# Gate and up products of the five FFNs: one 512-column matmul over high and low activations in place of two of 256

## The reference, cut to what matters

```python
def swiglu(h, w_gate, w_up, w_down):          # D_MODEL = 1024, D_FF = 2816, four times
    return (jax.nn.silu(h @ w_gate) * (h @ w_up)) @ w_down
...
        h = _causal_depthwise_conv(x @ w_up[l], conv_w[l], conv_b[l])   # 3 taps, once
        a, u = jnp.split(h, 2, axis=-1)
        ffn = (jax.nn.gelu(a, approximate=False) * u) @ w_down[l]
```

## Time and profile before

| | us |
|---|---|
| timed runs, median of 3 | 1504.58 (1501.1 to 1508.84) |
| span of the profiled execution | 1502.6 |
| TensorE matmuls busy in it | 1390.1 |
| VectorE busy | 883.2 |
| ScalarE busy | 641.9 |

### The profile page before, as it was taken

The page is one execution under the profiler, slowest core; times in us unless marked ns, Lnnn a source line. Parts: engine busy times, 40 slices in busy tenths (PEclk is TensorE's granted clock), DMA queues, the critical chain, the costliest instruction groups (busy, mean ns, idle before and its releaser), DMA issues.

```text
span 1502.6 us, 22505 instructions
## 1 busy us (share of the span) xinstructions
PE 1390.1 (93%) x9058; PEld 1276.6 (85%) x9058; DVE 883.2 (59%) x1146; ACT 641.9 (43%) x767; POOL 185.2 (12%) x196
## 2 busy tenths in 40 slices
PE   6999988898899989999889889999979999799996
PEld 6999976788799989999788769999968887699996
DVE  5445467765455565454556755445486747776667
ACT  4443443544343344434435544433436432354552
POOL 1100004008497000000000000000021310000000
PEclk9999998679999999999999999999989969899998
DMA  8755542229855536555454136555633322555551
GB/s 270 228 181 182 195 138 87 70 59 178 212 191 192 189 123 213 180 183 193 142 166 136 63 99 210 196 175 188 192 97 106 113 71 83 169 175 191 193 180 43
DMA packets 166339, 234.94 MB, mean 156 GB/s; under 512 B 4915, under 2 KB 134082, under 8 KB 166160
## 3 DMA queue, kind: packets, MB, share of 16 engines
q1 hardware_dynamic: 161792, 221.33, 45.6%
q0 software_dynamic: 4496, 12.91, 4.3%
HBM read 233.17 MB, written 1.05 MB: 156 GB/s over the span
## 4 chain that ended last, share of the span: by engine, by line
PE 84%; DVE 9%; ACT 2%; DMA 2%; issue 2%; SPq 0%; DVEq 0%; ACTq 0%
PE ps L304 27%; PE ps L305 26%; PE ps L306 26%; DMA raw<-in_ffn_w_gate_dram 2%; PE ps L834 1%; DVE w_lo L272 1%; PE ps L415 1%; PE ps L1460 1%; DMA raw<-in_ffn_w_up_dram 1%; ACT w_hi L264 1%; DVE h_lo L460 0%; DVE x_tok L1164 0%; DVE h_lo L977 0%; DVE p_sb L921 0%; DVE x_tok L1163 0%
## 5 line engine op out<-in xcount | busy, mean ns | idle before, releaser
L272 DVE TENSOR_TENSOR w_lo<-raw,w_hi 128x2048 fp32r<-128x2048 f32 x209 | 487.1, 2334 | 281.1 <-ACT w_hi L264 281.0
L304 PE MATMUL ps<-h_hi,w_hi 128*128 128x256 f32 x2016 | 578.3, 287 | 12.7 <-DVE w_lo L272 5.0
L305 PE MATMUL ps<-h_hi,w_lo 128*128 128x256 f32 x2016 | 576.0, 286 | 0.0
L306 PE MATMUL ps<-h_lo,w_hi 128*128 128x256 f32 x2016 | 575.7, 286 | 0.0
L264 ACT ACTIVATE w_hi<-raw 128x2048 fp32r<-128x2048 f32 x209 | 398.9, 1910 | 334.3 <-PE ps L306 301.4
L304 PEld LDWEIGHTS ps<-h_hi,w_hi 128*128 128x128 f32 x2016 | 392.9, 195 | 18.5 <-issue 10.8
L305 PEld LDWEIGHTS ps<-h_hi,w_lo 128*128 128x128 f32 x2016 | 393.0, 195 | 1.7
L306 PEld LDWEIGHTS ps<-h_lo,w_hi 128*128 128x128 f32 x2016 | 392.5, 195 | 0.0
L304 PE MATMUL ps<-w_hi,gu_hi 128*128 128x512 f32 x400 | 156.3, 391 | 1.2 <-DVE w_lo L272 1.2
L305 PE MATMUL ps<-w_hi,gu_lo 128*128 128x512 f32 x400 | 156.2, 391 | 0.0
L306 PE MATMUL ps<-w_lo,gu_hi 128*128 128x512 f32 x400 | 155.6, 389 | 0.0
(11 more groups left out here) (249 smaller groups left out, 1311.1 us busy)
## 6 DMA issues: line engine op xcount, KB each, us to landing
raw<-in_ffn_w_gate_dram SPq DMA_DIRECT2D x44, 1024.0 KB, 5.3
raw<-in_ffn_w_up_dram SPq DMA_DIRECT2D x44, 1024.0 KB, 5.4
raw<-in_ffn_w_down_dram SPq DMA_DIRECT2D x44, 1024.0 KB, 4.9
raw<-in_w_up_dram SPq DMA_DIRECT2D x22, 1024.0 KB, 5.1
raw<-in_w_in_dram SPq DMA_DIRECT2D x14, 1024.0 KB, 5.3
raw<-in_odd_w_qkv_dram SPq DMA_DIRECT2D x12, 1024.0 KB, 5.2
raw<-in_w_down_dram SPq DMA_DIRECT2D x11, 1024.0 KB, 4.9
raw<-in_even_w_in_dram SPq DMA_DIRECT2D x6, 1024.0 KB, 5.2
```

The costliest lines, as they stand in the source:

```text
L272: dve.tensor_tensor(w_lo[slot][:, :], raw[slot][:, :], w_hi[slot][:, :].bitcast(F32), ALU.subtract).then_inc(w_lo_ready, 1)
L304: mm(o, ahi, bhi, start=first, stop=False)
L305: mm(o, alo, bhi, start=False, stop=False)
L306: return mm(o, ahi, blo, start=False, stop=last)
```

## The change

h_hi and h_lo become two halves of one tile, h_both, so that one matmul can stream both: 256 columns of hi, then 256 of lo. In the FFNs' gate and up units a new `wide_unit` replaces `feat_unit`. Per (t, k) it streams h_both through the high weights into a whole bank of 512 columns, and h_hi through the low weights into that bank's first half. A bank's two halves must then be added. ScalarE copies the second halves of two banks (t = 0 and 1) to SBUF (`act_part`), and VectorE adds the first halves to them (`dve_sum`). Gate takes banks 0 and 1, up takes 2 and 3. In the plain FFNs gate's sum is in ffn_part (p_sb's second half) and up's in ffn_up; in the conv FFN both go through ffn_part, and all taps read it there instead of PSUM. The order of the splits is changed round these. The projections keep `feat_unit`.

```diff
-        h_hi = sb("h_hi", [P, KC, S], F32R)
-        h_lo = sb("h_lo", [P, KC, S], F32R)
+        h_both = sb("h_both", [P, 2, KC, S], F32R)
+        h_hi, h_lo = h_both[:, 0], h_both[:, 1]
...
+        def wide_unit(pe, n, banks, i=0, ready=None):
...
+            for t in range(2):
+                for k in range(KC):
...
+                    pe.matmul(PS[:, banks + t, :], a[:, k, f], h_both[:, :, k, :], start=k == 0, stop=False)
+                    last = pe.matmul(PS[:, banks + t, 0:S], b[:, k, f], h_hi[:, k, :], start=False, stop=k == KC - 1)
+            last.then_inc(w_released, 1)
...
                 if free is not None:
-                    if self.conv:
-                        pe.wait_ge(self.a_conv if which == 0 else self.u_conv, free)
-                    else:
-                        pe.wait_ge(self.act_done if which == 0 else self.gu_done, free + self.b)
-                feat_unit(pe, n, which, i)
...
+                    pe.wait_ge(self.summed, 2 * free + (2 * self.b + which - 1))
+                wide_unit(pe, n, 2 * which, i)
+
+            def act_part(self, act, which, i, at, dst):
...
                 act.wait_ge(w_released, self.u0 + 1 + which + at)
+                act.activation(dst.rearrange("p (t s) -> p t s", t=2), PS[:, 2 * which:2 * which + 2, S:2 * S], ACT.Copy)\
+                   .then_inc(self.part_ready, 1)
+
+            def dve_sum(self, dve, which, i, part):
+
+                dve.wait_ge(self.part_ready, 2 * i + (2 * self.b + which + 1))
+                p = part.rearrange("p (t s) -> p t s", t=2)
+                dve.tensor_tensor(p, PS[:, 2 * which:2 * which + 2, 0:S], p, ALU.add).then_inc(self.summed, 1)
...
+                at = 0 if first else 3 * r + 2
+                if not first:
                     split_hi(act, u + 4, i=r)
+                if self.conv and not first:
+                    act.wait_ge(self.u_conv, i)
+                self.act_part(act, 0, i, at, ffn_part)
+                split_hi(act, u + 2 if first else u + 5, i=r)
                 if self.conv:
...
+                    self.conv_tap2(act, 0, i)
                     act.wait_ge(self.a_conv, i + 1)
                     act.activation(ffn_act, ffn_act, ACT.Gelu).then_inc(self.act_done, 1)
+                    self.act_part(act, 1, i, at, ffn_part)
                 else:
...
+                    act.wait_ge(self.summed, 2 * i + (2 * self.b + 1))
+                    act.activation(ffn_act, ffn_part, ACT.Silu).then_inc(self.act_done, 1)
+
+                    if not first:
+                        act.wait_ge(self.gu_done, i + self.b)
+                    self.act_part(act, 1, i, at, ffn_up)
+                last = isinstance(i, int) and i == FF_STEPS - 1
+                if not last:
+                    split_hi(act, u + 3 if first else u + 6, i=r)
+                if self.conv:
+                    self.conv_tap2(act, 1, i)
...
+                if last:
+                    split_hi(act, u + 6, i=r)
```

More of the change, by code:

```diff
@@ L176, in build @@
         ffn_gu = p_sb[:, 0, :]
+        ffn_part = p_sb[:, 1, :]
         PJ = arena[:, 0:3072].rearrange("p (t n) -> p t n", t=TB)
@@ L319, in feat_unit @@
                                  h_hi[:, k, :], h_lo[:, k, :], k == 0, k == KC - 1)
+            last.then_inc(w_released, 1)
+        def wide_unit(pe, n, banks, i=0, ready=None):
+            slot = n % RING
+            pe.wait_ge(w_lo_ready, 3 * i + (n + 1))
+            a, b = feat_view(w_hi[slot]), feat_view(w_lo[slot])
+            for t in range(2):
+                for k in range(KC):
+                    if ready is not None and t == 0:
+                        ready(pe, k)
+                    f = slice(t * P, (t + 1) * P)
+                    pe.matmul(PS[:, banks + t, :], a[:, k, f], h_both[:, :, k, :], start=k == 0, stop=False)
+                    last = pe.matmul(PS[:, banks + t, 0:S], b[:, k, f], h_hi[:, k, :], start=False, stop=k == KC - 1)
             last.then_inc(w_released, 1)
@@ L466, in build @@
         class Ffn:
+            part_ready = sem("ffn_part_ready")
+            summed = sem("ffn_summed")
             act_done = sem("ffn_act_done")
@@ L531, in conv_tap2 @@
                     tile = i * 2 + (22 * which + t)
-                    m = act.activation(dst[:, t * S:(t + 1) * S], PS[:, which, t * S:(t + 1) * S], ACT.Identity,
+                    m = act.activation(dst[:, t * S:(t + 1) * S], ffn_part[:, t * S:(t + 1) * S], ACT.Identity,
                                        bias=convc[:, 3, bass.ds(tile, 1)], scale=convc[:, 2, bass.ds(tile, 1)])
@@ L542, in conv_taps @@
                     y = dst[:, t * S + 1:(t + 1) * S]
-                    m = dve.scalar_tensor_tensor(y, PS[:, which, t * S:(t + 1) * S - 1],
+                    m = dve.scalar_tensor_tensor(y, ffn_part[:, t * S:(t + 1) * S - 1],
                                                  convc[:, 1, bass.ds(tile, 1)], y, ALU.mult, ALU.add)
@@ L549, in conv_taps @@
                     y = dst[:, t * S + 2:(t + 1) * S]
-                    m = dve.scalar_tensor_tensor(y, PS[:, which, t * S:(t + 1) * S - 2],
+                    m = dve.scalar_tensor_tensor(y, ffn_part[:, t * S:(t + 1) * S - 2],
                                                  convc[:, 0, bass.ds(tile, 1)], y, ALU.mult, ALU.add)
@@ L557, in act_step @@
                 u, r = self.u0, (0 if first else i - 1)
[L558 to L563, removed]
+                at = 0 if first else 3 * r + 2
+                if not first:
                     split_hi(act, u + 4, i=r)
+                if self.conv and not first:
+                    act.wait_ge(self.u_conv, i)
+                self.act_part(act, 0, i, at, ffn_part)
+                split_hi(act, u + 2 if first else u + 5, i=r)
                 if self.conv:
[L566 to L569, removed]
+                    self.conv_tap2(act, 0, i)
                     act.wait_ge(self.a_conv, i + 1)
                     act.activation(ffn_act, ffn_act, ACT.Gelu).then_inc(self.act_done, 1)
+                    self.act_part(act, 1, i, at, ffn_part)
                 else:
[L574 to L577, removed]
+                    act.wait_ge(self.summed, 2 * i + (2 * self.b + 1))
[8 more added lines that the diff above has]
+                    self.conv_tap2(act, 1, i)
                 act.wait_ge(self.gu_done, i + (self.b + 1))
-                last = isinstance(i, int) and i == FF_STEPS - 1
                 if last:
@@ L601, in dve_step @@
                 u, r = self.u0, (0 if first else i - 1)
-                split_lo(dve, u + 2 if first else u + 4, i=r)
+                last = isinstance(i, int) and i == FF_STEPS - 1
+                if not first:
+                    split_lo(dve, u + 4, i=r)
+                self.dve_sum(dve, 0, i, ffn_part)
+                split_lo(dve, u + 2 if first else u + 5, i=r)
                 if self.conv:
                     self.conv_taps(dve, 0, i)
-                split_lo(dve, u + 3 if first else u + 5, i=r)
-                if self.conv:
+                    self.dve_sum(dve, 1, i, ffn_part)
+                    if not last:
+                        split_lo(dve, u + 3 if first else u + 6, i=r)
                     self.conv_taps(dve, 1, i)
                     dve.wait_ge(self.u_conv, i + 1)
[L609 to L612, removed]
-                else:
[L615 to L620, removed]
+                else:
+                    self.dve_sum(dve, 1, i, ffn_up)
+                    dve.wait_ge(self.summed, 2 * i + (2 * self.b + 2))
+                dve.wait_ge(self.act_done, i + (self.b + 1))
                 if not first:
-                    split_lo(dve, u + 6, i=r)
+                    dve.wait_ge(self.gulo_done, i + self.b)
+                dve.tensor_tensor(ffn_gu, ffn_up, ffn_act, ALU.mult).then_inc(self.gu_done, 1)
+                if not self.conv and not last:
+                    split_lo(dve, u + 3 if first else u + 6, i=r)
                 dve.wait_ge(self.guhi_done, i + (self.b + 1))
-                last = isinstance(i, int) and i == FF_STEPS - 1
                 hi, lo = (h_hi[:, 0:2, :], h_lo[:, 0:2, :]) if last else (gu_hi[:, :, :], gu_lo[:, :, :])
@@ L627, in dve_step @@
                    .then_inc(self.gulo_done, 1)
+                if last:
+                    split_lo(dve, u + 6, i=r)
             def dve(self, dve, then=None):
```

5 lines of the change are left out of this document (3 added, 2 removed).

## The result

The changed kernel took 1516.02 us (median of 4 runs, 1514.89 to 1517.36) beside 1505.36 for the kernel before (4 runs, 1501.1 to 1508.84): a ratio of 1.0076, 95% interval 1.0055 to 1.0097. It is slower by 0.8%, and lies outside the predicted range of 1492 to 1513. Run again later it took 1515.16 us (6 runs) beside 1506.3: 1.0056, interval 1.0034 to 1.0078. One of the kernel before's later executions took 5798 us; it is left out of all ratios and ranges here.

What follows compares the result with a forecast made beforehand. It took TensorE to bound the kernel, and ScalarE and VectorE the changed conv FFN. Plain FFNs -17.0 and conv FFN +14.7 gave -2.3 us from 1504.6, put as 1502.5 us, range 1492 to 1513.

Steps and rivals of the forecast that it cites:

- The pair's saving: FFN gate and up units on TensorE: one weight load and matmul fewer per (t, k), 13.1 ns less, 360.0 to 346.9.
- my case's own range: Whole kernel, the prediction's main case, chance 0.64: 1497 to 1510 us, from conv bounds 10 to 19 and a few ns.
- Rival B: Wide matmuls: the stream in two pieces costs about 11 ns, only some 2.5 ns saved, 1516 us; chance 0.08.
- A: Wide and narrow matmuls: weight load hides wholly under the long stream, 26 ns saved, 1486 us; chance 0.11.
- D: Conv FFN: chain isn't the bound since ScalarE runs ahead, only its end is lost, 1492 us; chance 0.06.
- C: Conv FFN: chain longer than added up, 18.4 us a step, ten steps add 10 us, 1512.5 us; chance 0.11.
- The conv FFN: Conv FFN section: step bound by ScalarE and VectorE at 17.4 us, 14.7 us more in all, bounds 10 and 19.
- the last wait: End of the conv FFN: uncovered chain of 11.7 us makes the last down unit start 6.3 us late.
- the two waits at the start: Start of the conv FFN on TensorE: second up unit waits 1.0 us, first down unit 1.9 us.
- the clock: Conv FFN after its last wait: half a cold stretch at 1.2 GHz added, 2.5 us (1.7 to 2.8).
- The copies and adds of the plain FFNs: Plain FFN steps: two ScalarE copies and two VectorE adds lie under TensorE's work and cost nothing.
- the stall: ffn2_0: TensorE's wait for w_lo behind late weight loads, some 7 us instead of 6.2.

Runs made afterwards that it cites:

- second pair of profiles: Changed kernel and kernel before, both profiled again unaltered: spans 1513.9 and 1505.9 us; ratio of that pair's runs 1.0056.
- two and two: Changed kernel with its matmuls ordered two wide, two narrow instead of alternating singly: 1509.2 us, one run.

## Why the prediction was wrong

**The pair's saving is the step that failed** (What the change saves on TensorE): 13.1 ns per (t, k) measured 6.7, 360.0 less 353.3. The plain steps gained 0.19 us in place of 0.42, the plain FFNs 8.5 us in place of 17.0 (6.8 in the second pair of profiles). That alone makes 8.5 of the 12.4 us between forecast difference and measured spans. The bounds of 0 and 26 held it, but my case's own range gave the term only "a few ns". The reason was in the trace of before, a few rows ahead of those I used. I priced 512 columns from 112.33 on the earlier trace rows, in the middle of a run of wide matmuls. Its start, directly behind 256-column ones, reads:

```profile
110.72 0.40 PE L304 MATMUL ps<-w_hi,gu_hi 128*128 128x512 f32 x1
110.95 0.40 PE L305 MATMUL ps<-w_hi,gu_lo 128*128 128x512 f32 x1
111.19 0.39 PE L306 MATMUL ps<-w_lo,gu_hi 128*128 128x512 f32 x1
...
112.11 0.39 PE L304 MATMUL ps<-w_hi,gu_hi 128*128 128x512 f32 x1
```

Six take 1.39 us, 0.232 each: unrounded 233, 236, 228, 233, 230, 227 ns. The changed kernel puts every wide matmul into that situation. Pricing them from these rows, at 233 + 120 ns, would have given 353 ns a pair, 7 saved, and a forecast some 8 us higher. The sum would have been better than its parts: one by one the wide ones take 236 on average and the narrow ones 117.

**Rival B** named nearly the measured time, 1516, and a small saving, but its mechanism, the stream in two pieces, is refuted, and its saving of 2.5 ns was too small. The time agrees by luck, because the other sections' 4 us came on top. **A** needed 26 ns saved, which didn't happen; **D** said that the chain doesn't bind, and it does; **C** put the conv step at 18.4 us, and it is 17.5.

**The conv FFN was foretold nearly right**, as a sum: +14.7 against +14.5, the step 17.4 against 17.5 us, the last wait 6.3 against 5.7. The terms are less exact. The waits of TensorE add to 5.7 + 5.5 + 0.6 = 11.8 us and not 16.8: TensorE's own step is 16.79, which leaves 0.3 to 0.5 us of idle time a step where 0.85 was forecast, and the two waits at the start are 0.6 and 1.4 instead of 1.0 and 1.9. But a wait costs 0.16 us more than its idle time, since without one the next matmul starts 0.16 us before the row of the one before ends. By the distances between starts the twelve waits cost 13.7 us. The last one, after a matmul that starts at 1486.92:

```profile
1486.92 0.39 PE L308 MATMUL ps<-w_lo,gu_hi 128*128 128x512 f32 x1
1492.99 0.79 PE L306 MATMUL ps<-w_hi,h_both 128*128 128x512 f32 x1 [5.68 <-DVE h_both L658]
1493.59 0.63 PE L307 MATMUL ps<-w_hi,h_both 128*128 128x512 f32 x1
1494.01 0.63 PE L308 MATMUL ps<-w_lo,h_both 128*128 128x512 f32 x1
```

I put the clock at 2.5 us. The rows behind 1492.99 are at half clock. The conv FFN has 11 us of it, 3 before, but 3 of the 11 pass within the last wait and cost nothing; the matmuls that run at half clock cost 2.3 us more than before. Those at full clock take 1.4 us less and not 4.6: 2.4 us are saved in the pairs, and 1.1 lost again by the first matmul behind each wait, which takes 0.1 us more than its like (334 ns at 1359.11, where 227 is usual). 13.7 + 2.3 - 1.4 = 14.6, against 14.5 in the table by rounding. The total came so near because the waits and the matmuls' saving were both put too high. Of what holds up's copy the working named the shared buffer and the queue; it took both changes to open the loop.

**The other steps.** The copies and adds of the plain FFNs lie under TensorE's work, as said: with 16.57 us a step and 16.0 of the 17.0 us in the four FFNs, nearly all of the forecast gain is there once the order is right. In ffn2_0 the stall was forecast at 7 us, and reads 6.8 + 0.3 us:

```profile
PE ps L334 <- DVE w_lo L274: 6.8, 1, 6.8
PE ps L306 <- DVE w_lo L274: 0.3, 1, 0.3
```

**The sections outside** were taken at 0 with no width. They moved by 4.0 us between single profiles. The sum was made against one profile of 1502.6 us, which had a favourable clock: the second one spans 1505.9, and later medians of the kernel before are 1506.3 to 1507.1, against the 1504.6 from which the forecast started: some 2 us too low.

## What to carry to other kernels

Price an instruction from the rows where its neighbours are those it will have after the change: the same 512-column matmul took 226.7 ns among its like and 232 to 240 ns between 256-column ones. Where a change merges such matmuls, don't alternate: here the wide ones of a unit together and the narrow ones behind them gave the shortest step, 16.57 us, and two and two was nearly as good, 16.59. Where a step gets a new wait on an in-order engine, look at what is queued behind the waiting instruction and whether it can go first: here one copy ahead of gelu, together with the second buffer that allows it, turned a loss of 14.5 us into one of about 1, and the second buffer without it gave nothing. And take the spread of sections that a change leaves alone into the range: 4 us here between two profiles.

## What the runs showed of the hardware

Matmuls on fresh weights at the full clock of 2.4 GHz settle at 120.0 ns for 256 columns and 226.7 for 512. Behind narrow ones the first five wide ones take 234, 235, 229, 232, 231 ns, and the first narrow one behind wide ones 113. One by one a pair takes 353.3 ns, two by two 348.3, in long runs 346.7 plus some 20 ns for each run of wide ones (27 lost at its start, 7 won behind it). Back-to-back issue gap in TensorE: Matmul & The Clock Gate of the Trainium skill gives N/2.4 + 2.5 ns for the warm gap of a single, isolated matmul, 109.2 and 215.8 ns. No distance here came down to it at either size, the shortest being 112 and 224 ns, and the neighbour's size mattered too. An input stream in two pieces of 256 columns, apart in SBUF, gave the same step as one piece, 16.79 us.

The clock of a section can differ from run to run of an unaltered kernel: in the odd attention section, where TensorE was busy for 15 to 17 us in 20, it spent 16 us at 1.2 GHz in one profile and 36 us in another. The spans of 46 runs of the kernel before went from 1500.2 to 1511.9 us.
